# Key lookup by TensorE, gates written in eight pieces, a later choice and a rounded output projection in one transformer step

## The chip, the cores and the metric

One core of a Trainium2 chip runs the whole program. The metric is device time in microseconds (us) of one execution.

## The reference, cut to what matters

There are 640 tokens: 128 of a prompt and 512 latent ("sample") tokens, in five blocks of 128; block 0 is the prompt. Each group goes through one layer: normalisation and modulation, an input projection, differential attention (half of the width) and Fourier mixing (the other half), an output projection into the residual, and then a retrieval over 16384 single-neuron experts.

```python
x = x + g1 * mixer_merge(att, four, subln_g, lam_init, w_out)   # m @ w_out, m of 1024 columns
h2 = rmsnorm(x, norm2_g) * (1 + sc2) + sh2
q = (hf @ w_query).reshape(T, N_PEER_HEADS, 2, PEER_KEY_DIM // 2)
s = jnp.einsum('thpk,hpnk->thpn', q, sub_keys)
s1, i1 = lax.top_k(s[:, :, 0], PEER_TOPK)
s2, i2 = lax.top_k(s[:, :, 1], PEER_TOPK)
cand = s1[..., :, None] + s2[..., None, :]
top_s, pos = lax.top_k(cand.reshape(T, 8, 256), PEER_TOPK)
idx = (i1 * 128 + i2) at pos
g = softmax(top_s)
a = gelu(einsum('tkd,td->tk', expert_u[idx], hx))
out = einsum('tk,tkd->td', g * a, expert_v[idx])
```

Every token thus picks 16 experts for each of 8 heads, 128 in all, each named by two keys of 128 (i1, the row of the expert table, and i2, the column).

## The kernel before

Engines are named PE (TensorE), DVE (VectorE), ACT (ScalarE), POOL (GpSimd) and SP (SyncE, which issues most transfers). Each engine has its own program, written out by hand in order, and they meet at semaphores (`s_...`). The stages of the profiled execution:

- **Modulation and input projection** (0 to 209 us). The projection `z` is done in three products of rounded numbers: a number is split into `hi` (rounded to the type fp32r) and `lo` (the rest), and hi*hi, hi*lo and lo*hi are summed (L1599, L1600, L1603). The output projection is not done so: it is one plain f32 product.
- **Fourier mixing** (209 to 235): eight units; ACT copies each result into `mixT`.
- **Attention** (235 to 311): 20 iterations, one for each block and head, the prompt's four first. DVE takes maxima (L1132), scales and combines; ACT does exponentials and, in `att_out`, copies the turned output into `mixT` (L798); POOL does a `pow` for each block.
- **Merges** (311 to 386). `merge(b, half)` on PE (L1758) multiplies block b of `mixT` with a half (512 columns) of the output weights, 8 matmuls for each of ten pairs. DVE multiplies the result with the gate (L1192) and adds it to X (L1194); ACT squares X for the norm (`square2`, L824); DVE prepares the variance (`make_h2`, L1180), POOL raises it to the power (L512), and DVE makes h2 in two operations (L1182, L1184). PE turns h2 (`turned`, L1767), ACT rounds it (`turned_high`, L837) and DVE takes the rest (`turned_low`). The order is staggered: blocks 0 to 2 are merged wholly before the first turn. Meanwhile the query weights are split: ACT `query_high` (L830), DVE `query_low` for chunks 0 and 1 (L1208), POOL for 2 and 3 (L586).
- **Query projection and key scores** (386 to 554). PE runs `products3` (L1784 to L1786). DVE finds the top 16 keys of each head and side (`key_tops`). POOL builds a table `curve` in L590.
- **Choice of block 1** (554 to 568), then **three gate blocks** starting at 568.24, 612.62 and 657.04 and ending at 706.8. For the three dense blocks (ORDER is 1, 2, 3, 4, 0; the first three are dense) the gates of all 16384 experts are laid out as a matrix in memory (`gates_scratch`). For 32 groups of four tokens (quads), PE forms differences between token keys and all keys (`differences`, L1860), ACT makes them a one-hot operand (`one_hot`, L867), DVE makes the other operand (`gate_rows`, L1386; every fourth on POOL, L557), PE multiplies them (`dense_gates`, L1873), and ACT copies the result out (L905). SP sends half a block at a time to memory; of the last half, first 8 of 64 pairs (512 KB) and then the other 56 in one transfer (3584 KB).
- While block n is laid out, DVE also **chooses** for the next one (`choose`): sums of pairs (L1255), candidates, ranks (`select`). The keys at the ranks are looked up so: `is_equal` against all ranks gives a one-hot (L1350), a multiplication puts the index in (L1352), and a tree of additions over 16 places sums it up (L1356, L1357), once for each side. DVE then writes the key, its square and the rest of its square as `key2` (L1360 to L1363). PE spreads these in `stack_fill` (after quad 24 of the block before), ACT copies them (`stack_out`, p of 25), PE turns keys and gates (`selT_fill`, after quad 27; ACT `sel_out` at p of 28).
- **Into the experts** (706.8 to 739.5). DVE chooses for the prompt (`choose(4, 0, 0, 0, (0, 0))`); SP loads the first gates back; the pipeline of expert pairs starts up.
- **Experts** (to 1765), 128 steps: for the dense blocks, PE computes scores of 128 experts against 384 tokens (`U_hi`, `U_lo`), ACT the gelu, DVE multiplies with the gates (L1441), and PE the product with V (L1784 to L1786 again). The other two blocks (4 and the prompt) are done by POOL, which fetches rows one by one (L537), and DVE, which multiplies them (L1459, L1470). X, spilled to memory before, comes back in the course of it, and a tail ends the program.

Lines that the text touches, as they stand before:

```python
            choose(0, 0, 0, 0, (0, 0))
            choose(1, 1, 2, 3, (2, 6))
            choose(2, 2, 2, 3, (2, 6))
            choose(3, 3, 2, 3, (2, 0))
```

The numbers in `choose` say how many quads of the running block DVE does between the parts of a choice: 18 before `gate_weights` and 6 behind it.

Of the kernel before, what the change touches and what calls it, by code (L numbers as in the profile page):

```python
# [15 lines left out]
H = 4  # L16
# [21 lines left out]
SPARSE = (4, 0)  # L38
RPB = 4
# [12 lines left out]
GCUT = (0, 8, PAIRS)  # L52
# [21 lines left out]
def _phase1_jobs():  # L74
# [18 lines left out]
    for i, u in enumerate(units):  # L93
        jobs += [(("fa",) + u, "act"), (("fb",) + u, "dve")]
        if i:
            jobs.append((("fmix",) + units[i - 1], "act"))
    jobs.append((("fmix",) + units[-1], "act"))
# [4 lines left out]
def _phase2_jobs():  # L102

    order = ["m0", "m1", "m2", "T0", "m3", "T1", ("merge", 4, 0), "T2", ("merge", 4, 1), "T3", "T4"]
    jobs = []
    for o in order:
        if isinstance(o, tuple):
            jobs.append((o, "dve"))
        else:
            kind = "merge" if o[0] == "m" else "h2T"  # L110
            jobs += [((kind, int(o[1]), half), "dve") for half in range(2)]
    return jobs
# [19 lines left out]
def program(nc, xall, condT, w_mod, b_mod, norm1_g, w_in, lam4, subln_g, w_fourier, w_out, norm2_g,  # L132
# [7 lines left out]
    with ctx:  # L140
# [41 lines left out]
        with ExitStack() as over:  # L182
# [8 lines left out]
            wq_lo_first = laid("wq_lo_first", [P, KD, NC], f32r)  # L191
        w_hi = [w_hi_first] + [w_hi_next] * (IN_CH - 1)
# [20 lines left out]
        mixT = cutout(WO + WRING * KD * NC, 5120).rearrange("p (k t) -> p k t", k=KD)  # L213
# [7 lines left out]
        wq_in = [cutout(CO + 10240, KD * NC).rearrange("p (k n) -> p k n", k=KD)] + [chunk[:, r] for r in (0, 2, 1)]  # L221
        wq_hi = [wq_hi_even, wq_hi_odd] * 2
        wq_lo = [wq_lo_first[:, :, :]] + [w_lo[:, r] for r in (0, 2, 1)]
# [5 lines left out]
        onehot = cutout(BO + 4096, 1024).bitcast(bf16).rearrange("p (j s) -> p j s", j=TOPK)  # L229
# [15 lines left out]
        square = cutout(BO + 4096, P)  # L245
# [75 lines left out]
        s_arstd = sem("s_arstd"); s_att = sem("s_att"); s_attT = sem("s_attT"); s_mix = sem("s_mix")  # L321
        s_fill2 = sem("s_fill2"); s_h2hi = sem("s_h2hi"); s_dve2 = sem("s_dve2")
# [5 lines left out]
        s_selT = sem("s_selT"); s_selfill = sem("s_selfill"); s_diff = sem("s_diff"); s_key2 = sem("s_key2"); s_stackfill = sem("s_stackfill"); s_stack = sem("s_stack"); s_curve = sem("s_curve"); s_tab = sem("s_tab"); s_lhs1 = sem("s_lhs1"); s_rhs1 = sem("s_rhs1"); s_rhs1p = sem("s_rhs1p")  # L328
# [14 lines left out]
        DFT_C = MOD_CH + IN_CH  # L343
        OUT_C = DFT_C + 1
        CHUNKS = OUT_C + OUT_CH
# [20 lines left out]
        def _(sp):  # L366
# [23 lines left out]
            sp.wait_ge(s_mix, NBLK)  # L390
# [37 lines left out]
            for b in range(1, NDEN + 1):  # L428
                for half in range(2):
# [12 lines left out]
                    for r in range(len(GCUT) - 1):  # L442
                        pairs = slice(GCUT[r], GCUT[r + 1])
                        sp.dma_start(to[:, pairs], held[:, pairs]).then_inc(s_gpart[r], 16)
# [20 lines left out]
            load_pairs(1, GCUT[1] // 2)  # L465
            sp.wait_ge(s_gpart[1], 16)
            sp.wait_ge(s_spill, 16 * NBLK)
            at = [GCUT[1] // 2] + [2 * NBLK + 3 * b for b in range(NBLK + 1)] + [TWICE]
            for b in range(NBLK + 1):
                load_pairs(at[b], at[b + 1])  # L470
                if b < NBLK:
                    sp.dma_start(XF[:, b], x1_d[b * P:(b + 1) * P, :]).then_inc(s_xf, 16)
                else:
                    sp.dma_start(fing, final_g.unsqueeze(0).broadcast_to([P, D])).then_inc(s_fing, 16)
# [1511 lines left out]
```

## Time and profile before

| | us |
|---|---|
| median of three runs | 1820.45 (1818.86 to 1822.13) |
| the profiled execution | 1815.94 |
| its span (first to last instruction) | 1813.9 |
| mean granted clock of TensorE | 0.966 of full speed |

Rows of a timeline give the start, the duration and the instruction (a run of alike ones is one row with its count), and in brackets how long the engine was idle before it and what released it. Groups by line give busy time, mean ns of one, and idle time before. A row by source gives minimum, median and maximum ns. The window rows give, for each engine, its busy time and the number of instructions in the stretch.

### The profile page before, as it was taken

The page shows a single profiled execution, that of the slowest core. Times are in us where ns is not written, and L with a number is a line of the kernel's source. Part 1 is how long each engine was busy: PE and PEld are TensorE (multiplying, and loading weights), DVE is VectorE, ACT ScalarE, POOL GpSimd, SP SyncE. Part 2 cuts the span into 40 slices and gives each one's busy share as a digit, 9 for nine tenths or more (in the row PEclk, how much of TensorE's full clock was granted, in tenths as well). Part 3 has the DMA queues.
Part 4 walks back from the last instruction along what each step waited for, and adds up shares of the span by engine and source line. Part 5 has one row for each costly group of instructions (what it writes and reads, how often), then busy time and mean ns, then how long its engine had stood idle before and what let it go on. Part 6 is the DMA issues. An engine that isn't in the chain of part 4 may idle for free.

```text
span 1813.9 us, 28223 instructions
## 1 busy us (share of the span) xinstructions
PE 1665.3 (92%) x9322; PEld 1442.0 (79%) x9338; DVE 1506.1 (83%) x3069; ACT 645.6 (36%) x1085; POOL 916.1 (51%) x771
## 2 busy tenths in 40 slices
PE   4999998999954886899999999999999999999994
PEld 2776766479953886799999999999999999999993
DVE  0732266457999999799999999999999999999997
ACT  1212266121103785233333333333333333333331
POOL 1101000013402665777778877777666666666661
PEclk9999999999976998999999999999999999999997
DMA  9445202140010668999999999999999999999993
GB/s 355 173 163 208 75 1 98 42 184 3 1 47 1 187 186 253 385 406 409 407 408 390 402 409 409 409 409 409 409 408 409 409 409 403 410 409 407 406 397 124
DMA packets 198137, 518.28 MB, mean 286 GB/s; under 512 B 14643, under 2 KB 64435, under 8 KB 197941
## 3 DMA queue, kind: packets, MB, share of 16 engines
q0 software_dynamic: 73728, 268.47, 37.3%
q1 hardware_dynamic: 122320, 245.59, 36.3%
q10 hardware_dynamic: 2022, 3.38, 0.5%
q8 instruction: 36, 0.59, 0.1%
q14 instruction: 31, 0.25, 0.0%
HBM read 486.45 MB, written 30.93 MB: 285 GB/s over the span
## 4 chain that ended last, share of the span: by engine, by line
PE 79%; DVE 10%; DMA 5%; issue 3%; ACT 3%; POOL 0%; SPq 0%; POOLq 0%; ACTq 0%; DVEq 0%; PEldq 0%; another core or an unknown queue 0%
PE ps L1786 20%; PE ps L1785 20%; PE ps L1784 19%; PE ps L1758 4%; PE ps L1873 4%; DMA arena_w<-in_w_mod 2%; PE ps L1599 2%; PE ps L1603 2%; PE ps L1600 2%; PE ps L1697 2%; DMA arena_w<-in_w_in 1%; ACT arena_w L867 1%; DVE arena L1470 1%; PE ps L1721 1%; DVE arena L1307 1%
## 5 line engine op out<-in xcount | busy, mean ns | idle before, releaser
L1786 PE MATMUL ps<-hT_hi,U_lo 128*128 128x384 f32 x1024 | 344.3, 336 | 0.0
L1784 PE MATMUL ps<-hT_hi,U_hi 128*128 128x384 f32 x1024 | 344.1, 336 | 0.0
L1785 PE MATMUL ps<-hT_lo,U_hi 128*128 128x384 f32 x1024 | 343.5, 335 | 0.0
L537 POOL DMA_INDIRECT rows_under<-in_expert_u,idxn x192 | 273.8, 1426 | 116.4 <-issue 41.8
L1784 PE MATMUL ps<-hT_hi,C_hi 128*128 128x512 f32 x768 | 301.2, 392 | 14.5 <-DVE C_lo L1447 14.5
L537 POOL DMA_INDIRECT rows_under<-in_expert_v,idxn x192 | 242.7, 1264 | 140.4 <-DVE arena L1470 77.8
L1786 PE MATMUL ps<-hT_hi,C_lo 128*128 128x512 f32 x768 | 303.2, 395 | 0.0
L1785 PE MATMUL ps<-hT_lo,C_hi 128*128 128x512 f32 x768 | 303.1, 395 | 0.0
L1470 DVE SCALAR_TENSOR_TENSOR arena<-rows_under,dots,arena 128x1024 f32<-128x1024 f32 x192 | 247.8, 1291 | 4.8
L930 ACT ACTIVATE act_t<-ps 128x384 f32<-128x384 f32 x128 | 63.0, 492 | 386.2 <-PE ps L1786 386.2
L1784 PEld LDWEIGHTS ps<-hT_hi,U_hi 128*128 128x128 f32 x1024 | 192.6, 188 | 4.9
L1785 PEld LDWEIGHTS ps<-hT_lo,U_hi 128*128 128x128 f32 x1024 | 192.4, 188 | 4.9
L892 ACT CAST hT_hi<-arena 128x1024 fp32r<-128x1024 f32 x128 | 135.0, 1055 | 170.7 <-PE ps L1786 170.6
L1786 PEld LDWEIGHTS ps<-hT_hi,U_lo 128*128 128x128 f32 x1024 | 192.3, 188 | 0.0
L1784 PEld LDWEIGHTS ps<-hT_hi,C_hi 128*128 128x128 f32 x768 | 145.6, 190 | 42.9 <-DVE C_lo L1447 15.6
L1408 DVE TENSOR_TENSOR U_lo<-U_in,U_hi 128x1024 fp32r<-128x1024 f32 x128 | 156.3, 1222 | 21.5 <-ACT U_hi L885 21.2
L1786 PEld LDWEIGHTS ps<-hT_hi,C_lo 128*128 128x128 f32 x768 | 145.2, 189 | 30.7
L1785 PEld LDWEIGHTS ps<-hT_lo,C_hi 128*128 128x128 f32 x768 | 145.3, 189 | 27.7
L885 ACT CAST U_hi<-U_in 128x1024 fp32r<-128x1024 f32 x128 | 134.1, 1048 | 80.7 <-DMA U_in<-in_expert_uT 80.4
L1413 DVE TENSOR_TENSOR hT_lo<-arena,hT_hi 128x1024 fp32r<-128x1024 f32 x128 | 155.8, 1217 | 2.9 <-ACT hT_hi L892 2.8
L557 POOL TENSOR_SCALAR arena<-iota,arena 128x128 f32<-128x128 f32 x96 | 90.8, 955 | 127.7 <-ACT arena L876 81.0
L1459 DVE SCALAR_TENSOR_TENSOR rows_under<-rows_under,arena_w 128x1024 f32<-128x1024 f32 x96 | 116.0, 1220 | 7.7 <-DMA rows_under<-in_expert_u,idxn 7.7
(273 smaller groups left out, 3010.9 us busy)
## 6 DMA issues: line engine op xcount, KB each, us to landing
U_in<-in_expert_uT SPq DMA_DIRECT2D x128, 512.0 KB, 8.7
arena<-in_expert_v SPq DMA_DIRECT2D x128, 512.0 KB, 6.5
arena_w<-in_w_mod SPq DMA_DIRECT2D x12, 2048.0 KB, 12.4
gate_in<-gates_scratch SPq DMA_DIRECT2D x62, 384.0 KB, 7.9
gates_scratch<-arena_w SPq DMA_DIRECT2D x5, 4096.0 KB, 16.6
arena_w<-in_w_in SPq DMA_DIRECT2D x4, 2048.0 KB, 8.7
arena_w<-in_w_query SPq DMA_DIRECT2D x4, 2048.0 KB, 10.8
arena_w<-in_w_out SPq DMA_DIRECT2D x2, 2048.0 KB, 8.4
```

Source lines behind the costliest of these rows:

```text
L537: pool.indirect_dma_start(out=rowr[row], out_offset=None, in_=table, in_offset=bass.IndirectOffsetOnAxis(ap=idxn[:, g, row:row + 1], axis= ...
L557: ins = pool.tensor_scalar(rhs1[AIDED][:, t, :], iota[:, :], selT[:, b % 2, 0, at:at + 1], selT[:, b % 2, 1, at:at + 1], ALU.is_equal, ALU ...
L885: act.copy(U_hi[:, r], U_in[:, r]).then_inc(s_uhi, 1)
L892: act.copy(V_hi[r], V_in[:, r].rearrange("p (k n) -> p k n", k=KD)).then_inc(s_vhi, 1)
L1408: dve.tensor_tensor(U_lo[:, r], U_in[:, r], U_hi[:, r].bitcast(f32), ALU.subtract).then_inc(s_ulo, 1)
L1413: dve.tensor_tensor(V_lo[r], V_in[:, r].rearrange("p (k n) -> p k n", k=KD), V_hi[r].bitcast(f32), ALU.subtract).then_inc(s_vlo, 1)
L1459: dve.scalar_tensor_tensor(out=rowr[q], in0=rowr[q], scalar=1.0, in1=h2row[k], op0=ALU.mult, op1=ALU.mult, accum_out=dst).then_inc(s_used, 1)
L1470: dve.scalar_tensor_tensor(out=accS[:, k], in0=rowr[q], scalar=c, in1=accS[:, k], op0=ALU.mult, op1=ALU.add).then_inc(s_used, 1)
L1758: last = nc.tensor.matmul(out, mixT[:, k, b * P:(b + 1) * P], chunk[:, (OUT_C + half) % WRING, k, :], start=(k == 0), stop=(k == KD - 1))
L1784: nc.tensor.matmul(out, hi, rhi, start=start, stop=False)
L1785: nc.tensor.matmul(out, hi, rlo, start=False, stop=False)
L1786: return nc.tensor.matmul(out, lo, rhi, start=False, stop=stop)
```

## The change

1. **Output projection in three rounded products.** `mixT` becomes `mix_hi` and `mix_lo`, the weights `wo_hi` and `wo_lo`; PE does 24 matmuls for each `merge` in place of 8. New work: ACT `out_high` (16 casts, eight of them in the prompt's four attention iterations), POOL `out_low` (8 before the attention's `pow`s, 8 behind), DVE `mix_low` (8, after the Fourier units) and `att_low` (5, in the attention loop; PE waits for it). All first halves are merged before any second half; a block's h2 is made after its second half. `query_low` of chunk 0 moves from DVE to POOL, and the load of chunk 0 waits for the first five merges.
2. **Key lookup on PE.** For the first four choices the tree of additions gives way to `pick`: 16 accumulating matmuls of 128 x 128 x 128 in bf16 with a unit matrix, once for each side, after quads 16 and 21 of the block. ACT makes the squares (`key_squares`, after quad 23), DVE only the rest (`finish`, ahead of its last 6 quads, waiting for ACT's `s_keysq`). `stack_fill` comes two quads later.
3. **Gates in pieces.** The last half block is written in eight transfers of 512 KB; only the first goes out at once, the others between the loads of turns 2 to 18 of the expert loop. POOL's third row fetch waits for one gate load less. The loads that bring X back come a turn or two earlier.
4. **The prompt's choice parted.** Its candidates and first side stay ahead of the experts; its second side and its weights move into the first expert step.

```diff
-GCUT = (0, 8, PAIRS)
+GCUT = tuple(range(0, PAIRS + 1, 8))
+SENT = {1: 2, 2: 4, 3: 6, 4: 8, 5: 12, 6: 15, 7: 18}
+BACK = {0: 9, 1: 11, 2: 14, 3: 17, 4: 20, NBLK: 23}
...
-    order = ["m0", "m1", "m2", "T0", "m3", "T1", ("merge", 4, 0), "T2", ("merge", 4, 1), "T3", "T4"]
...
+    jobs = [(("merge", b, 0), "dve") for b in range(NBLK)]
+    for b in range(NBLK):
+        jobs.append((("merge", b, 1), "dve"))
+        jobs += [(("h2T", b - 1, half), "dve") for half in range(2 if b else 0)]
+    jobs += [(("h2T", NBLK - 1, half), "dve") for half in range(2)]
...
-        mixT = cutout(WO + WRING * KD * NC, 5120).rearrange("p (k t) -> p k t", k=KD)
+        mix_hi = HT_lo
+        mix_lo = HT_hi[:, :, :].rearrange("p k t -> p (k t)").rearrange("p (b k t) -> p b k t", b=NBLK, k=KD)
+        wo_hi = [w_lo[:, DFT_C % WRING], wq_lo_first[:, :, :]]
+        wo_lo = [w_lo[:, (OUT_C + half) % WRING] for half in range(OUT_CH)]
...
+            sp.wait_ge(s_fill2, NBLK)
             sp.dma_start(wq_in[0], w_query_v[:, :, 0:NC]).then_inc(s_wq[0], 16)
             for b in range(NBLK):
-                sp.wait_ge(s_x1, 2 * (b + 1))
+                sp.wait_ge(s_x1, NBLK + b + 1)
...
+                    sp.dma_start(to[:, 0:GCUT[1]], held[:, 0:GCUT[1]]).then_inc(s_gpart[0], 16)
+            def send_part(r):
+                pairs = slice(GCUT[r], GCUT[r + 1])
+                sp.dma_start(gates_d[pairs, :, 2 * NDEN - 1].rearrange("m p e t -> p m (e t)"),
+                             gbuf[:, 1].rearrange("p (m e) t -> p m (e t)", e=2)[:, pairs]).then_inc(s_gpart[r], 16)
...
+            turn = 1
+            for at in sorted(set(SENT.values()) | set(BACK.values())) + [TWICE]:
+                for r in range(1, len(GCUT) - 1):
+                    if turn < 4 * r < at:
+                        load_pairs(turn, 4 * r)
+                        turn = 4 * r
+                    if turn == 4 * r:
+                        sp.wait_ge(s_gpart[r], 16)
+                load_pairs(turn, at)
+                turn = at
+                for r in SENT:
+                    if SENT[r] == at:
+                        send_part(r)
...
+            def out_low(half):
+                src = chunk[:, (OUT_C + half) % WRING]
+                for k in range(KD):
+                    pool.wait_ge(s_ohi, KD * half + k + 1)
+                    pool.tensor_tensor(wo_lo[half][:, k, :], src[:, k, :], wo_hi[half][:, k, :].bitcast(f32),
+                                       ALU.subtract).then_inc(s_olo, 1)
...
+            out_low(0)
             for b in range(NBLK):
                 pool.wait_ge(s_avar, b + 1)
                 pool.tensor_tensor(ss4[:, 1, :], ss4[:, 0, :], powe[:, 0:H], ALU.pow).then_inc(s_arstd, 1)
+            out_low(1)
             for b in range(NBLK):
+                if b == NBLK - 1:
+                    query_low(0, range(2 * b - 2, 2 * b))
...
                 if first and row == 2:
-                    for part in s_gin:
-                        pool.wait_ge(part, 16)
+                    pool.wait_ge(s_gin[0], 16)
...
                 if ci == 2:
+                    pool.wait_ge(s_qfill, 16)
...
+                for k in ks:
+                    act.copy(wo_hi[half][:, k, :], chunk[:, i % WRING, k, :]).then_inc(s_ohi, 1)
...
+                if i < KD // 2:
+                    out_high(0, range(2 * i, 2 * i + 2))
+            out_high(1, range(KD))
...
+            for b in range(1, NBLK):
+                if b == NBLK - 1:
+                    act.wait_ge(s_fill2, B2.pos["merge", b, 1] + 1)
+                    query_high(0, range(2 * b - 2, 2 * b))
+                square2(b)
+                turned_high(b - 1)
+                if b < NBLK - 1:
+                    query_high(0, range(2 * b - 2, 2 * b))
+            turned_high(NBLK - 1)
...
+            def key_squares(n):
+                act.wait_ge(s_picked, 2 * n + 2)
+                if n:
+                    act.wait_ge(s_stackfill, n)
+                    act.wait_ge(s_key2, n)
+                act.copy(key2[:, 0, :], ps[:, 0, 256:384]).then_inc(s_keysq0, 1)
+                act.activation(square, ps[:, 0, 256:384], ACT.Square).then_inc(s_keysq0, 1)
+                act.wait_ge(s_keysq0, 2 * n + 2)
+                act.copy(key2[:, 1, :], square).then_inc(s_keysq, 1)
...
+                    key_squares(b)
+                if b < NDEN and p == 27:
...
+                src = bank1("fmix", s, g)
+                dve.wait_ge(s_fhi, units.index(u) + 1)
+                if s == 0:
+                    dve.tensor_tensor(mix_lo[:, 0, 4 + g, :], src[:, 0:P], mix_hi[:, 4 + g, 0:P].bitcast(f32),
+                                      ALU.subtract).then_inc(s_dve1, 1)
+                else:
...
+                if i:
+                    mix_low(units[i - 1])
+            mix_low(units[-1])
...
+            def att_low(b):
+                dve.wait_ge(s_mix, b + 1)
+                dve.scalar_tensor_tensor(out=mix_lo[:, b, 0:4, :], in0=ps[:, 7, :].rearrange("p (h t) -> p h t", h=H),
+                                         scalar=lam[:, 7:8], in1=mix_hi[:, 0:4, b * P:(b + 1) * P].bitcast(f32),
+                                         op0=ALU.mult, op1=ALU.subtract).then_inc(s_mixlo, 1)
...
+            dve.wait_ge(s_out, 32)
+            for b in range(NBLK):
+                merge(b, 0)
+            for b in range(NBLK):
+                merge(b, 1)
+                var2(b)
+                if b:
+                    turned_low(b - 1)
+                make_h2(b)
+            turned_low(NBLK - 1)
...
+            def picked(n, ws, bd=0, share=(0, 0, 0, 0)):
+                b = ORDER[n]
...
+                    if n and n < LATE_PICK:
+                        dve.wait_ge(s_picked, 2 * n - 1 + w)
...
+                    eqs = dve.tensor_tensor(o4, o4, idxf[:, w].unsqueeze(2).broadcast_to([P, TOPK, TOPK, PH]), ALU.mult)
+                    if n < LATE_PICK:
+                        eqs.then_inc(s_eqs, 1)
+                        gate_quads(bd, share[2 * w + 1])
+                        continue
...
+            def finish(n):
                 if n < NDEN:
...
-                    link(dve.tensor_copy(key2[:, 1, :], square))
+                    dve.wait_ge(s_keysq, n + 1)
                     dve.tensor_tensor(key2[:, 2, :], square, key2[:, 1, :], ALU.subtract).then_inc(s_key2, 1)
...
+                candidates(n, bd, pairs_share)
+                picked(n, (0, 1), bd, (select_share,) * 4)
                 gate_quads(bd, weights_share[0])
                 gate_weights(n)
+                finish(n)
                 gate_quads(bd, weights_share[1])
...
+            candidates(4, 0, 0)
+            picked(4, (0,))
+            def first_row(i, q):
+                if i == 0 and q == 2:
+                    picked(4, (1,))
+                    gate_weights(4)
+                dot_row(0)(i, q)
...
-                    pe.wait_ge(s_mix, b)
+                    pe.wait_ge(s_mixlo, b)
...
+                    if b == 0:
+                        pe.wait_ge(s_olo, KD * half + k + 1)
+                    last = products3(out, mix_hi[:, k, b * P:(b + 1) * P], mix_lo[:, b, k, :],
+                                     wo_hi[half][:, k, :], wo_lo[half][:, k, :], k == 0, k == KD - 1)
...
+            for b in range(NBLK):
+                merge(b, 0)
+            for b in range(NBLK):
+                merge(b, 1)
+                if b:
+                    turned(b - 1)
...
+            def pick(n, w):
...
+                if n and w == 0:
+                    pe.wait_ge(s_selT, n)
+                if n and w == 1:
+                    pe.wait_ge(s_keysq, n)
+                for j in range(TOPK):
+                    if w == 0 and n < NDEN:
+                        last = nc.tensor.matmul(ps[:, 0, 0:P], onehots[0][:, j, :], identb, start=(j == 0), stop=(j == TOPK - 1))
+                    else:
+                        at = 256 if w else 384
+                        last = nc.tensor.matmul(ps[:, 0, at:at + P], identb, onehots[w][:, j, :],
+                                                start=(j == 0), stop=(j == TOPK - 1))
+                last.then_inc(s_picked, 1)
...
+            pick(0, 0)
+            pick(0, 1)
...
+                if q % QUADS in (16, 21):
+                    pick(q // QUADS + 1, (q % QUADS - 16) // 5)
+                if q % QUADS == 26 and q // QUADS + 1 < NDEN:
```

## Rows read from the trace of the kernel before

**Rows 1.** The page: its first line and the busy time of each engine.
```profile
span 1813.9 us, 28223 instructions
...
PE 1665.3 (92%) x9322; PEld 1442.0 (79%) x9338; DVE 1506.1 (83%) x3069; ACT 645.6 (36%) x1085; POOL 916.1 (51%) x771
```
**Rows 2.** Busy time in four windows: attention, merges, first gate block, experts.
```profile
core 0: us, PE busy (x) PEld busy (x) DVE busy (x) ACT busy (x) POOL busy (x), PEclk, DMA share, GB/s
240.00:300.00 60.00, 57.21 (x355) 44.06 (x355) 53.01 (x108) 44.47 (x134) 3.54 (x3) 0.96 0.00 1
311.06:385.90 74.84, 74.84 (x193) 34.81 (x193) 31.48 (x45) 11.72 (x22) 2.17 (x4) 0.96 0.15 57
568.24:612.62 44.38, 39.17 (x284) 35.08 (x289) 41.33 (x145) 33.74 (x65) 29.04 (x32) 0.91 0.34 96
1300.00:1350.00 50.00, 50.00 (x254) 45.55 (x253) 48.90 (x50) 18.12 (x25) 31.64 (x27) 1.00 1.03 408
```
**Rows 3.** PE's timeline: products of the merges, rounded products of the input projection.
```profile
start us, us, engine line op out<-in xcount [idle before <-releaser]
...
311.06 44.11 PE L1758 MATMUL ps<-arena_w 128*128 128x512 f32 x96 [0.78 <-ACT arena_w L800]
...
185.68 0.39 PE L1599 MATMUL ps<-w_hi_next,HT_hi 128*128 128x512 f32 x1
...
208.57 0.39 PE L1603 MATMUL ps<-w_lo,HT_hi 128*128 128x512 f32 x1
```
**Rows 4.** Timeline, DVE and ACT at the end of the merges.
```profile
385.31 0.69 DVE L1192 TENSOR_TENSOR arena_w<-ps,arena 128x512 f32<-128x512 f32 x1 [3.82 <-PE ps L1758]
...
386.75 1.06 ACT L824 ACTIVATE arena_w<-arena 128x1024 f32<-128x1024 f32 x1 [7.68 <-DVE arena L1194]
...
388.74 1.34 DVE L1182 SCALAR_TENSOR_TENSOR arena_w<-arena,rstd 128x1024 f32<-128x1024 f32 x1 [0.65 <-POOL rstd L512]
...
390.11 1.31 DVE L1184 TENSOR_TENSOR arena_w<-arena_w,arena 128x1024 f32<-128x1024 f32 x1
```
**Rows 5.** Timeline of POOL and DVE at 439 us; L1255 and L586 by source.
```profile
439.16 7.03 POOL L590 TENSOR_TENSOR arena_w<-ident,arena_w 32x4096 bf16<-32x4096 f32 x1
...
442.10 4.14 DVE L1255 TENSOR_TENSOR arena<-arena 128x32 f32<-128x32 f32 x1
...
L1255 DVE TENSOR_TENSOR arena<-arena x20: 163/171/4145, 442.1 to 702.4; 128x32 f32<-128x32 f32 x20
...
L586 POOL TENSOR_TENSOR w_lo<-arena_w,wq_hi_even x8: 1281/1288/1301, 424.3 to 437.8; 128x512 fp32r<-128x512 f32 x8
```
**Rows 6.** Groups of instructions by line, the whole span.
```profile
L1062 DVE TENSOR_TENSOR HT_lo<-ps,HT_hi 128x512 fp32r<-128x512 f32 x10 | 6.4, 682 | 0.7 <-ACT HT_hi L684 0.7
...
L867 ACT ACTIVATE arena_w<-ps 128x512 f32<-128x512 f32 x96 | 58.3, 608 | 0.4 <-PE ps L1860 0.2 <-remote 0.2
...
L905 ACT COPY arena_w<-ps 128x512 f32<-128x512 f32 x96 | 56.5, 589 | 31.7 <-PE ps L1873 30.3
...
L1356 DVE TENSOR_TENSOR arena<-arena 128x1024 bf16<-128x1024 bf16 (+2 forms) x30 | 14.8, 494 | 0.8
```
**Rows 7.** Timeline of the second gate block, 612 to 658 us.
```profile
623.24 1.71 PE L1873 MATMUL ps<-arena_w 128*128 128x128 f32 x8 [2.69 <-issue]
...
625.16 1.92 PE L1873 MATMUL ps<-rhs_more,arena_w 128*128 128x128 f32 x8
...
633.38 4.45 POOL L557 TENSOR_SCALAR arena<-iota,arena 128x128 f32<-128x128 f32 x4 [1.33 <-PE ps L1873]
...
635.39 0.31 ACT L880 ACTIVATE arena<-arena 128x128 f32<-128x128 f32 x1
...
647.57 2.14 DVE L1386 TENSOR_SCALAR arena_w<-iota,arena 128x128 f32<-128x128 f32 x8
...
648.28 1.05 PE L1873 MATMUL ps<-arena,arena_w 128*128 128x128 f32 x8
...
649.38 1.05 PE L1873 MATMUL ps<-arena_w 128*128 128x128 f32 x8
```
**Rows 8.** The way into the experts: DVE and PE timeline, and one DMA issue.
```profile
719.21 0.56 DVE L1441 TENSOR_TENSOR act_t<-act_t,gate_in 128x384 f32<-128x384 f32 x1 [1.28 <-DMA gate_in<-gates_scratch]
...
739.49 0.67 PE L1784 MATMUL ps<-hT_hi,C_hi 128*128 128x512 f32 x1 [4.55 <-DVE C_lo L1447]
...
gates_scratch<-arena_w SPq DMA_DIRECT2D x1, 3584.0 KB, 22.2
```

More of the change, by code:

```diff
@@ L38 @@
 SPARSE = (4, 0)
+LATE_PICK = 4
 RPB = 4
@@ L95, in _phase1_jobs @@
         if i:
-            jobs.append((("fmix",) + units[i - 1], "act"))
-    jobs.append((("fmix",) + units[-1], "act"))
+            jobs.append((("fmix",) + units[i - 1], "dve"))
+    jobs.append((("fmix",) + units[-1], "dve"))
     return jobs
 def _phase2_jobs():
-    order = ["m0", "m1", "m2", "T0", "m3", "T1", ("merge", 4, 0), "T2", ("merge", 4, 1), "T3", "T4"]
[L105 to L111, printed above, removed]
+    jobs = [(("merge", b, 0), "dve") for b in range(NBLK)]
[3 more added lines that the diff above has]
+    jobs += [(("h2T", NBLK - 1, half), "dve") for half in range(2)]
     return jobs
@@ L894, in _ @@
             share_exps(0)
+            key_squares(0)
             stack_out(1)
@@ L1169, in _ @@
                     att_norm(i // H - 2)
+                if i % H == 2 and i > 2 * H:
+                    att_low(i // H - 2)
             def bank2(*name):
@@ L1749, in bank2, with products3 @@
                 return ps[:, i % 8, :]
-            pe.wait_ge(s_mix, NBLK)
+            pe.wait_ge(s_mixlo, NBLK)
             pe.wait_ge(s_exp, 2 * len(UNITS))
-            chunk_ready(OUT_C)
-            chunk_ready(OUT_C + 1)
+            def products3(out, hi, lo, rhi, rlo, start, stop):
+                nc.tensor.matmul(out, hi, rhi, start=start, stop=False)
+                nc.tensor.matmul(out, hi, rlo, start=False, stop=False)
+                return nc.tensor.matmul(out, lo, rhi, start=False, stop=stop)
             def merge(b, half):
@@ L1757, in merge @@
                 for k in range(KD):
-                    last = nc.tensor.matmul(out, mixT[:, k, b * P:(b + 1) * P], chunk[:, (OUT_C + half) % WRING, k, :],
-                                            start=(k == 0), stop=(k == KD - 1))
+                    if b == 0:
+                        pe.wait_ge(s_olo, KD * half + k + 1)
+                    last = products3(out, mix_hi[:, k, b * P:(b + 1) * P], mix_lo[:, b, k, :],
+                                     wo_hi[half][:, k, :], wo_lo[half][:, k, :], k == 0, k == KD - 1)
                 last.then_inc(s_fill2, 1)
@@ L1848, in selT_fill @@
                     pe.wait_ge(s_selT, b - 1)
-                for w, src in enumerate((sel[:, 0, :], gates[:, 1, :])):
-                    last = nc.tensor.transpose(ps[:, 0, w * P:(w + 1) * P], src, ident[:, :])
-                last.then_inc(s_selfill, 1)
+                nc.tensor.transpose(ps[:, 0, P:2 * P], gates[:, 1, :], ident[:, :]).then_inc(s_selfill, 1)
             def differences(q):
```

195 lines of the change are left out of this document (85 added, 110 removed).

## The prediction

> **What bounds the kernel now.** I read the page first. The span is 1813.9 us, PE is busy for 92% of it and DVE for 83% [rows 1]; a share like this is a mean over stages, so the windows come next. In the experts PE never idles (50.00 of 50.00 us), and DMA is at a share of 1.03 and DVE at 48.90 of 50 [rows 2]: there only PE work removed would count, and the change removes none. What it touches are the stages ahead. In attention PE is busy for 57.21 of 60 us and DVE for 53.01; in the merges PE for all of 74.84 us and DVE for only 31.48; in the first gate block of 44.38 us, PE for 39.17 and DVE for 41.33, so neither is full and the waits between them decide [rows 2]. The timelines of single engines in these stretches then give the durations.
>
> **1. Attention and Fourier.** The change puts eight DVE operations behind the Fourier units; all but the last stand in DVE's gaps there, and the last is ahead of the first scores: one PSUM operation of 512 columns, 0.68 us [rows 6], +0.8 with its wait. `att_low` is five of that kind. Three stand in a loop in which DVE is idle 7 of 60 us: between 0 and 2.0, I take +1.0. One stands in the tail, where PE waits for it: +0.75. ACT's eight casts (0.61 each by the nearest row, 512 columns) stand in the prompt's short iterations: 4.9 us of work in a stage in which ACT is idle for 15 of 60; 0 to 3, I take +0.7. POOL's first eight `out_low` cost nothing as work (POOL is busy 3.54 of 60 us), but look at the rows around 442 us: while POOL's L590 ran from 439.16 to 446.19, DVE's L1255, usually 0.171 us, took 4.14 and ended just as POOL did [rows 5]. An operation of DVE on two SBUF inputs stood still until POOL's was over. Eight POOL operations of 1.29 us [rows 5] therefore can stop DVE eight times, by 0 to 10.3 us in all; on average a stop would be less than half an operation and not all meet such a DVE operation: +3.0 (0 to 7). Sum +6.25.
> The Trainium skill ("SBUF — State Buffer", section "SBUF: two separate sides") says that DVE and GpSimd share a pair of ports and that whichever starts first has it for the whole instruction, DVE only where it runs in a two-port mode or has two SBUF inputs. By that rule the maxima and other PSUM readers of the loop go on beside POOL, and this term would be nearer to +2; the trace agrees in the 4.14 us of an operation with two SBUF inputs.
>
> **2. Merges.** The 96 records of plain f32 are six halves of 16 (two records a matmul) and take 44.11 us [rows 3]; a half in the stage's steady part is 6.87 us, 0.43 a record, so that about 2.75 is the slow start. The rounded ones start every 0.2266 us: 101 intervals from 185.68 to 208.57 [rows 3]. 24 of them are 5.44 us for each half in place of 6.87. PE alone would need 10 x 5.44 + 4 x 0.9 (turns) + 2.75 = 60.8 us against 74.84. But the new order gives every block a chain behind its second half: from the multiplication at 385.31 over the square (1.06) and the variance to the end of h2 (1.34 + 1.31, done at 391.42) it is 6.1 us [rows 4]. I take 6.1 for the first and, with `turned_low` of the block before in between, about 7.0 for the next three, where PE needs 6.4. So: 2.75 + 6 x 5.44 = 35.4 to the end of the sixth half, then 6.1 + 3 x 7.0 and the last turn, 63.8 in all: -11.0. Against this, POOL now does `query_low` of chunk 0 (2 x 1.29 for each block) while DVE makes h2 out of two SBUF inputs, the very pairing of the 4.14 us row: 0 to 9, I take three stops of 1.6 and a last of 0.7, +5.5. Net -5.5. Below -11 it can't come unless the chain is shorter than its rows.
>
> **3. Key stage.** Its work is the same. `query_low` of chunk 0 leaves DVE, and L590 comes later, with the same stop of DVE somewhere else (4.14 before). I take 0 (-2 to +4).
>
> **4. Gate stage.** The trees are 30 additions of 0.494 us [rows 6], six a choice, 3.0 us; with the last sum and the four key operations, each near the 0.31 of a 128-column one [rows 7], about 4.7 us of DVE for each choice. In the first choice PE is idle and DVE alone sets the pace: 4.7 less, and two picks, three ACT steps of 0.31 and hops more. A pick is 16 matmuls of 128 columns. A quad's eight f32 records of 128 columns take 1.05 us [rows 7], 0.13 each; a rounded matmul takes about half of a plain record (0.2266 to 0.43 above), so a pick is 1.05 to 2.1, and below that if bf16 is quicker still (0.9). I take 1.1 warm and twice that in this cold stretch. Net -1.0 (-1.6 to -0.6).
> The Trainium skill ("TensorE: Matmul & The Clock Gate", section "Wait — 56ns, not 53.3ns?") gives 55.6 ns for such a matmul at 2.4 GHz and 106.7 at 1.2; by it a pick would be 0.9 or 1.7 us, and the sum would stand within 0.5.
>
> In blocks 1 and 2 the gain doesn't arrive. Quads 11, 15, 19, 23 are bounded by POOL's own operand, made in up to 4.45 us [rows 7] after PE has freed a buffer; two picks of 1.1 fill what the trees leave. So quad 23 ends about when it does now, at 649.3. Now quad 24 starts at once, at 649.38 behind 648.28 [rows 7], since DVE had its operand ready. After the change DVE may not start this operand until `finish`, and `finish` waits for ACT's `key_squares`, which stand behind quad 23: ACT copies the result (0.59), makes a one-hot (0.61) [rows 6], then three steps of 0.31; DVE 0.3, then the quad's operand, half of the 2.14 us for two [rows 7], 1.07. That is 3.6 us with the overlap of the first two, plus 0.1 of a hop. Queued behind the waiting DVE are its last six quads and the next block's first, and PE waits for each. A gap of 2.69 us left the two next groups at 1.71 and 1.92 us in place of 1.05 [rows 7], which is the lower level of the clock, 1.2 GHz: +1.45 in two. Together +5.0 for each of two blocks (3.3 to 6). In block 3 `finish` waits for the picks alone, and the splits stand behind it: +1.5. Stage: +10.5.
>
> **5. Into the experts.** The first gates are used at 719.21, released by their load, and the second product with V starts at 739.49 after waits of PE [rows 8]. The load ran beside a transfer of 3584 KB that took 22.2 us [rows 8]; this goes, and the parted choice takes about 5 us of DVE out of the way, of which most comes back inside the first step. What then is late is DVE's chain of splits: I follow it to 17.6 us where it is 20.3 between the two rows, -2.7, and -2.3 for the load. -5.0 (-7 to -2).
>
> **6. Experts.** PE paces them, and the second part of the choice stands in a step in which DVE has a few us to spare. The seven pieces are 3584 KB, at 409 GB/s about 9 us of a DMA that is full [rows 2]; their cover is the loads' lead of a turn or more: 0, and +9 if that lead is gone.
>
> **Sum.** 6.25 - 5.5 + 0 + 10.5 - 5.0 = +6.25. The profiled execution took 1815.94 and would take 1822.2; it is 4.5 below the median of 1820.45, which becomes 1826.7.
>
> **Rivals.** (a) The gate blocks get shorter. If the chain behind quad 23 is covered, because operands for 24 and on are ready or ACT runs ahead, PE's work sets the block: 39.17 + 2.2 for the picks = 41.4 against 44.38, -3.0 in place of +5.0, twice: 1826.7 - 16 = 1810.7, faster. It decides once operand 24 is there by the end of 23. For it: DVE falls from 41.33 to about 36.6 us of the block. Against: the order of DVE's program. (b) The stops by POOL cost nothing, as both engines mostly read other operands: -3.0 - 5.5, so 1818.2. For it: among 20 L1255 one alone was slow [rows 5]. (c) DMA has no lead: +9, so 1835.7; the share of 1.03 speaks for it, PE's full 50 us against.
>
> **Chances.** Forecast 0.50 (own range 1820 to 1834), (a) 0.17, (b) 0.18, (c) 0.10, other 0.05. What can be told from no change is 0.2%, 3.6 us. The forecast lies 2.6 above that edge, so 0.40 of its 0.50 is slower and 0.09 within; (a) is nearly all faster; (b) is 0.06 faster, 0.09 within, 0.03 slower; (c) slower. That makes faster 0.24, within 0.20, slower 0.56. The range of 1809 to 1837 reaches from (a) to (c).
>
> **What would show it.** Merges: 24 matmuls in 5.44 us, a stage near 69 us, DVE rows of h2 over 1.34 beside POOL's 1.29. Gates: a PE idle of about 3 us before quad 24, released by DVE, and a period near 49 us; if the period is 41, (a) is right. Transition: PE's start on the second product with V less than 28 us after the end of the gates. Experts: 8.28 us a step as now. The prediction fails most easily at quad 24.

## Result and profile after

The changed kernel takes 1846.57 us (median of four runs, 1844.16 to 1856.2) against 1819.65 for the kernel before in the same runs; the ratio is 1.0162, with a 95% interval of 1.0141 to 1.0182. The forecast was 1826.7 with a range of 1809 to 1837: the sign was right and the size was not. Between the two profiled executions the difference is larger, 32.8 us where +6.25 was forecast, because the one before lies 3.7 us under that median and the one after 2.0 over its own.

The span of the profiled execution is 1846.7 us; it was 1813.9. The page's first line and its chain of work that ended last, by engine:

```profile
span 1846.7 us, 28485 instructions
...
PE 1680.0 (91%) x9525; PEld 1476.6 (80%) x9543; DVE 1506.1 (82%) x3035; ACT 651.8 (35%) x1110; POOL 947.7 (51%) x795
...
PE 56%; DMA 16%; DVE 15%; issue 7%; ACT 3%; POOL 2%; SPq 1%; DVEq 0%; POOLq 0%; another core or an unknown queue 0%; ACTq 0%; PEldq 0%
```

DMA is now 16% of the chain, where it was 5%. I cut both traces at the same five events of PE and took differences:

| stretch | before | after | difference | forecast |
|---|---|---|---|---|
| start to first product of the merges | 311.06 | 320.94 | +9.9 | +6.25 |
| merges, to the first query product | 74.84 | 68.16 | -6.7 | -5.5 |
| query, keys and first choice, to the first turn of gates | 181.21 | 179.10 | -2.1 | -1.0 |
| three gate blocks | 139.91 | 149.61 | +9.7 | +11.5 |
| into the experts, to the second product with V | 32.47 | 27.58 | -4.9 | -5.0 |
| from there to the end | 1074.41 | 1101.31 | +26.9 | 0 |

The first five sum to +5.9, for which +6.25 was forecast. The whole miss is the last line. The windows there (us, then busy time and count of PE, PEld, DVE, ACT and POOL, granted clock, DMA share, GB/s) answer to the last of [rows 2]:

```profile
740.00:790.00 50.00, 45.69 (x224) 40.86 (x222) 42.28 (x66) 15.56 (x22) 38.39 (x30) 0.97 0.98 376
1110.00:1160.00 50.00, 46.09 (x219) 41.15 (x218) 42.02 (x64) 15.35 (x21) 32.46 (x25) 0.93 0.98 379
1320.00:1370.00 50.00, 45.90 (x219) 41.20 (x218) 43.23 (x43) 14.88 (x21) 27.94 (x25) 0.93 0.98 382
```

Before, PE never idled between 740 and 1350 us. Now it loses 4 us in each window, and in the second and third its granted clock is 0.93. (In the first, 3.1 of the 4.3 us are still the way in: the second product with V starts at 745.39.) One such place, followed through the timelines of SP, ACT, DVE and PE, and then four windows of 4 us. U is the block of expert weights that a step loads; `U_hi` is its rounded part, made by ACT, and `U_lo` the rest, made by DVE; `C_hi` and `C_lo` are the same of the gated scores:

```profile
772.43 0.39 SPq L454 DMA_DIRECT2D gates_scratch<-arena_w  x1
773.19 0.69 SPq L423 DMA_DIRECT2D U_in<-in_expert_uT  x1
...
788.53 1.05 ACT L947 CAST U_hi<-U_in 128x1024 fp32r<-128x1024 f32 x1 [7.43 <-DMA U_in<-in_expert_uT]
789.48 0.51 ACT L999 CAST C_hi<-act_t 128x384 fp32r<-128x384 f32 x1
...
789.60 1.23 DVE L1517 TENSOR_TENSOR U_lo<-U_in,U_hi 128x1024 fp32r<-128x1024 f32 x1 [5.45 <-ACT U_hi L947]
...
792.50 0.50 PE L1872 MATMUL ps<-hT_hi,C_hi 128*128 128x512 f32 x1 [3.70 <-DVE C_lo L1564]
```

```profile
784.00:788.00 4.00, 4.00 (x24) 3.92 (x23) 0.16 (x2) 0.00 (x0) 3.03 (x4) 1.00 1.02 409
788.00:792.00 4.00, 0.80 (x5) 0.47 (x3) 2.40 (x4) 2.79 (x4) 0.00 (x0) 1.00 1.03 415
792.00:796.00 4.00, 3.50 (x10) 2.80 (x11) 4.00 (x7) 0.13 (x1) 2.91 (x2) 0.70 0.99 370
796.00:800.00 4.00, 4.00 (x19) 3.49 (x18) 4.00 (x7) 2.38 (x3) 3.39 (x3) 0.88 1.01 399
```

Read it upwards. PE is said to wait for `C_lo`, but DVE was idle from 784 to 788 (0.16 of 4 us): it stood at `U_lo`, which is ahead of `C_lo` in its program, for ACT's `U_hi`, and ACT had stood 7.43 us for the load of U. That load was issued at 773.19, in the same queue, right behind the piece sent at 772.43. After the idle, the granted clock is 0.70 and 0.88 in the next two windows: PE's first products still take 0.39 us, then those from 793.92 to 796.48 take 0.63, the lower of its levels, 1.2 GHz, and then it is back at 2.4. There are five such idles behind seven pieces, 3.70, 3.18, 3.91, 1.62 and 4.10 us, 16.5 in all. The same 610 us of experts, after and (from 740) before:

```profile
745.00:1355.00 610.00, 593.10 (x2940) 536.54 (x2941) 557.64 (x815) 207.62 (x279) 441.33 (x321) 0.98 1.01 396
```

```profile
740.00:1350.00 610.00, 610.00 (x3077) 555.29 (x3076) 582.02 (x840) 217.59 (x293) 455.51 (x332) 1.00 1.02 406
```

16.9 us are idle. PE has 2940 matmul records where it had 3077, which is 27.2 us of work at the old pace; so the other 10.3 us went into slower matmuls, and a mean clock of 0.98 (0.975 to 0.985) would take 9 to 15. The stalls and the slower work behind them make up the 26.9.

### The profile page after: what moved, and what is told of

Same layout as the page of the kernel before. It is cut to its first block, busy times and chain, and to the rows that moved or that the text cites. A ratio compares the mean times of both kernels' runs of the same rounds, so it can differ in the third digit from the quotient of the medians.

```text
span 1846.7 us, 28485 instructions
## 1 busy us (share of the span) xinstructions
PE 1680.0 (91%) x9525; PEld 1476.6 (80%) x9543; DVE 1506.1 (82%) x3035; ACT 651.8 (35%) x1110; POOL 947.7 (51%) x795
## 4 chain that ended last, share of the span: by engine, by line
PE 56%; DMA 16%; DVE 15%; issue 7%; ACT 3%; POOL 2%; SPq 1%; DVEq 0%; POOLq 0%; another core or an unknown queue 0%; ACTq 0%; PEldq 0%
PE ps L1872 13%; PE ps L1873 13%; PE ps L1874 13%; DMA U_in<-in_expert_uT 9%; PE ps L2000 4%; PE ps L1716 2%; PE ps L1720 2%; PE ps L1717 2%; DMA arena_w<-in_w_mod 2%; PE ps L1814 2%; POOL rows_under L583 2%; DMA arena_w<-in_w_in 1%; DVE hT_lo L1522 1%; DVE arena L1587 1%; DVE rows_under L1576 1%
## 5 line engine op out<-in xcount | busy, mean ns | idle before, releaser
L583 POOL DMA_INDIRECT rows_under<-in_expert_u,idxn x192 | 284.6, 1482 | 126.5 <-issue 52.6
L603 POOL TENSOR_SCALAR arena<-iota,arena 128x128 f32<-128x128 f32 x96 | 85.8, 904 | 140.2 <-ACT arena L938 78.8
```

What stands on the lines that cost most here:

```text
L583: pool.indirect_dma_start(out=rowr[row], out_offset=None, in_=table, in_offset=bass.IndirectOffsetOnAxis(ap=idxn[:, g, row:row + 1], axis= ...
L603: ins = pool.tensor_scalar(rhs1[AIDED][:, t, :], iota[:, :], selT[:, b % 2, 0, at:at + 1], selT[:, b % 2, 1, at:at + 1], ALU.is_equal, ALU ...
```

## Experiments

Ratios are to the kernel before, run beside each; it took 1816.2 to 1817.4 us there, so times are compared by their ratios. Lines of edits are against the changed kernel unless said otherwise.

**Two transfers again.**

```diff
-GCUT = tuple(range(0, PAIRS + 1, 8))
-SENT = {1: 2, 2: 4, 3: 6, 4: 8, 5: 12, 6: 15, 7: 18}
+GCUT = (0, 8, PAIRS)
+SENT = {}
...
-                    sp.dma_start(to[:, 0:GCUT[1]], held[:, 0:GCUT[1]]).then_inc(s_gpart[0], 16)
+                    for r in range(len(GCUT) - 1):
+                        pairs = slice(GCUT[r], GCUT[r + 1])
+                        sp.dma_start(to[:, pairs], held[:, pairs]).then_inc(s_gpart[r], 16)
```

> The changed kernel with the last half block of gates written in two transfers again (512 KB, then 3584 KB, both at the end of the gates); the earlier loads of X, POOL's earlier fetch and the parted choice stay. Theory A, the seven written pieces make the U loads late in the experts: no wait of PE of 3 us or more is left between the second product with V and the tail, that stretch falls from 1101.3 us to about 1075, and the time to 1825 to 1831 (26.9 less, up to 4.9 given back on the way into the experts). Theory B, it is the earlier X loads or the parted choice in the first step: the waits stay and the time is 1841 or more.

Measured 1823.83 us, ratio 1.0043 (1.0029 to 1.0057): 1.19% or 21.6 us better than the change. From the second product with V to the end it is 1077.3 us, and ahead of 1785 us one idle of 0.40 us is left in the experts. The earlier loads of X (also 512 KB each, in the same queue) and the parted choice are still in it, so theory B falls. (The edit also drops two waits of SP for pieces; the run with small packets below costs as much without any.) The way into the experts is 30.1 us: of the 4.9 gained there, half came from the pieces.

**Pieces alone,** on the kernel before: the same constants, `send_part`, SP's loop and POOL's third fetch.

> The kernel before with nothing but the gates in pieces (eight transfers, the moved loads of X, POOL's third fetch). Theory A: the experts lengthen by some 27 us, the way into them shortens by 0 to 5, so 1841 to 1847. Theory B (it takes the parted choice or a later start of the experts): within 4 us of 1819.7. Priced by bytes alone at 409 GB/s it would be +9, 1829.

Measured 1839.84 us, ratio 1.0134 (1.0117 to 1.0151), +24.3 us. PE waits for `C_lo` seven times between 745 and 1400 us, 18.6 us in all, up to 6.5. The pieces cost this without any other part.

**Half as large, twice as many.**

```diff
-GCUT = tuple(range(0, PAIRS + 1, 8))
-SENT = {1: 2, 2: 4, 3: 6, 4: 8, 5: 12, 6: 15, 7: 18}
+GCUT = (0,) + tuple(range(8, PAIRS + 1, 4))
+SENT = {r: r + 1 for r in range(1, 15)}
```

> The changed kernel with the same 3584 KB written in 14 pieces of 256 KB, one at each of turns 2 to 15, in place of 7 of 512 KB. If each write has to be longer than the lead of the U loads to be felt (a threshold), half a piece costs little and the time is under 1830. If the cost goes by bytes or packets written, it stays at 1843 to 1850.

Measured 1835.77 us, 1.0116 (1.0098 to 1.0133): neither. Against two transfers it still costs 13 us, against the full pieces it saves 8, for the same bytes in the same packets. The waits are smaller and more, ten with 12.1 us in all in place of five with 16.5 (its profiled execution, 1830.3 us, is the fastest of its four). That fits a slack in each step, as DVE and ACT run a little ahead, which takes up part of each burst; this is argued, not shown. Pieces of this size are in any case not free.

**Seven writes that nothing needs,** on the kernel with two transfers and the covered quad of the next experiment. A transfer moves its bytes in packets; the size of a packet follows from how long the stretches are that lie together at both ends. First in rows of 4096 bytes:

```diff
+EXTRA = (2, 4, 6, 8, 12, 15, 18)
...
+                if at in EXTRA:
+                    r = EXTRA.index(at)
+                    sp.dma_start(extra_d[r * P:(r + 1) * P, :], G2[:, 0]).then_inc(s_extra, 16)
```

> The kernel with two transfers and covered quad 24 (0.9988 of the time before), and seven further writes of 512 KB at the turns 2, 4, 6, 8, 12, 15 and 18, ahead of the same U loads as the pieces, but to a scratch tensor that nothing reads, in rows of 4096 bytes. If the cost of a piece is its small packets of 512 bytes, these cost little: within 8 us of that kernel. If any write of 512 KB in that place is the cost, PE waits 2 to 4 us behind most of them and the time is 15 to 27 us longer.

and in packets of 512 bytes, the only difference being how the same tensor is cut (the places in memory that one packet after the other goes to change with it). SP waits for these writes only at the very end:

```diff
-                    sp.dma_start(extra_d[r * P:(r + 1) * P, :], G2[:, 0]).then_inc(s_extra, 16)
+                    sp.dma_start(extra_d[r * P:(r + 1) * P, :].rearrange("(m c) d -> m (c d)", m=8).rearrange("m (p e) -> p m e", p=P),
+                                 G2[:, 0].rearrange("p (m e) -> p m e", m=8)).then_inc(s_extra, 16)
```

> The same seven scratch writes at the same turns, with the same bytes, but in packets of 512 bytes as the pieces have. Packets as the cause: 15 to 27 us longer than the kernel without them, with PE waits of 2 to 4 us. If bytes or writing are the cause: the same as the run with rows of 4096 bytes, whatever that is.

Rows: 1822.5 us, ratio 1.0023 (1.0011 to 1.0035). Small packets: 1842.19 us, 1.0136 (1.0119 to 1.0154). The kernel without either is at 0.9988. So 3584 KB more in packets of 4096 bytes cost 0.35%, 6.4 us, close to the 9 that bytes at 409 GB/s give, and in packets of 512 bytes 1.48%, 26.9 us. The DMA line of the page, rows first and small packets second, has the same bytes, and they differ by 6272 packets, which is 7 x (1024 - 128):

```profile
DMA packets 199148, 521.99 MB, mean 286 GB/s; under 512 B 14755, under 2 KB 64547, under 8 KB 198949
```

```profile
DMA packets 205420, 521.99 MB, mean 284 GB/s; under 512 B 14755, under 2 KB 71715, under 8 KB 205221
```

The waits between 740 and 1400 us (us in total, times, the longest), again rows first:

```profile
ACT U_hi L948 <- DMA U_in<-in_expert_uT: 210.7, 78, 4.4
...
PE ps L1873 <- DVE C_lo L1565: 1.3, 3, 0.6
```

```profile
ACT U_hi L948 <- DMA U_in<-in_expert_uT: 135.1, 48, 9.4
...
PE ps L1873 <- DVE C_lo L1565: 19.1, 8, 5.7
```

ACT waits for U longer in total with rows, but never for more than 4.4 us, and of that PE has only 1.3 us of waits; with small packets single waits reach 9.4. Between 760 and 1350 us PE does 2980 matmuls in the kernel without the writes, 2955 with rows and 2838 with small packets: 4.9 and 28.1 us of work at 0.198 us each. So most of the price of rows is not in waits of PE but in matmuls that run a little slower at a granted clock of 1.00, and the traces don't say why.

**Quad 24 covered** (with two transfers):

```diff
-            choose(1, 1, 2, 3, (2, 6))
-            choose(2, 2, 2, 3, (2, 6))
+            choose(1, 1, 2, 3, (4, 4))
+            choose(2, 2, 2, 3, (4, 4))
```

> As the run before (two parts), and in blocks 1 and 2 DVE builds its operands of quads 24 and 25 before finish, not behind it (shares 4 and 4 in place of 2 and 6). If the 3.29 us idle of PE ahead of quad 24 is DVE waiting for ACT's squares, both idles go and the gate stage is 6.5 to 10 us shorter than with two parts alone. Rival, DVE is short of time anyway and the wait only moves to a later quad: within 2 us of it.

Measured 1814.78 us, ratio 0.9988 (0.9977 to 1.0), 10 us better than with two transfers alone. The gate blocks fall from 149.6 to 141.9 us, which is still 2 more than before the change; the other 2 us of the 10 lie in small differences of the rest. In the changed kernel the place looked so (timeline of ACT, DVE and PE):

```profile
605.53 0.27 ACT L927 CAST arena<-ps 128x128 bf16<-128x128 f32 x1
605.68 0.31 ACT L928 ACTIVATE arena<-ps 128x128 f32<-128x128 f32 x1
606.02 0.30 ACT L930 CAST arena<-arena 128x128 bf16<-128x128 f32 x1
606.35 0.41 DVE L1461 TENSOR_TENSOR arena<-arena 128x128 bf16<-128x128 f32 x1 [6.29 <-ACT arena L930]
606.68 2.18 DVE L1487 TENSOR_SCALAR arena_w<-iota,arena 128x128 f32<-128x128 f32 x8
...
608.04 1.13 PE L2000 MATMUL ps<-arena_w 128*128 128x128 f32 x8 [3.29 <-issue]
...
609.22 1.88 PE L2000 MATMUL ps<-arena_w 128*128 128x128 f32 x8
...
611.32 1.70 PE L2000 MATMUL ps<-rhs_more,arena_w 128*128 128x128 f32 x8
```

DVE idled 6.29 us for ACT's three steps, with six operands still to make. With two of them made ahead, the idle of 3.29 is gone from both blocks:

```profile
602.37 1.05 PE L1998 MATMUL ps<-arena_w 128*128 128x128 f32 x8
603.26 0.38 PE L1985 MATMUL ps<-arena_w,arena 128*128 128x512 bf16 x1
604.72 1.13 PE L1998 MATMUL ps<-rhs_more,arena_w 128*128 128x128 f32 x8 [1.08 <-ACT arena_w L917]
```

**No rounded projection** (with two transfers and the covered quad): all of part 1 as in the kernel before.

> The kernel with two transfers and covered quad 24, without the rounded output projection (plain f32 products, the old order of the merges). By the traces the projection costs 7 us in attention and gives 7 back in the merges: within 3 us of 0.9988 of the time before. If the products are worth more than that, it is slower by 4 us or more.

Measured 1815.95 us, 0.9992 (0.998 to 1.0005). With and without it the time is the same within what can be told: it costs ahead of the merges what it gives in them.

**POOL's operations and DVE.** First, the low part of query chunk 0 on DVE, two pieces behind each block's h2:

```diff
                 make_h2(b)
+                if b:
+                    query_low(0, range(2 * b - 2, 2 * b))
```

> The kernel with two transfers and covered quad 24, with the low part of query chunk 0 made by DVE (0.69 us each, two behind each block's h2) and not by POOL. If POOL's 1.29 us operations hold DVE up (h2 in 2.21 and 2.17 us where the first block has 1.28 and 1.22), those fall back to about 1.3 and the merges get 1 to 5 us shorter (1.9 less and 1.4 more for each of three blocks, and the last block's 0.8). If DVE was slow for another reason, they stay above 2 and the merges are 4 to 6 us longer.

Measured 1819.05 us, 1.0006 (0.9996 to 1.0017), 3.3 us worse than 0.9988 (0.9977 to 1.0); the two intervals just touch. The operations did fall back. DVE's h2 of the first and the second block in the changed kernel, and of the second with this edit:

```profile
359.69 1.28 DVE L1275 SCALAR_TENSOR_TENSOR arena<-arena,rstd 128x1024 f32<-128x1024 f32 x1 [0.66 <-POOL rstd L557]
...
366.46 2.21 DVE L1275 SCALAR_TENSOR_TENSOR arena_w<-arena,rstd 128x1024 f32<-128x1024 f32 x1
368.70 2.17 DVE L1277 TENSOR_TENSOR arena_w<-arena_w,arena 128x1024 f32<-128x1024 f32 x1
```

```profile
366.37 1.27 DVE L1269 SCALAR_TENSOR_TENSOR arena_w<-arena,rstd 128x1024 f32<-128x1024 f32 x1
367.68 1.23 DVE L1271 TENSOR_TENSOR arena_w<-arena_w,arena 128x1024 f32<-128x1024 f32 x1
...
392.71 1.52 DVE L1296 TENSOR_TENSOR w_lo<-arena_w,wq_hi_even 128x512 fp32r<-128x512 f32 x2
```

The merges got 2.4 us shorter (67.4 to 65.0), but the last pair of the chunk stood behind the last h2, done at 394; PE waited 5.1 us for it, and query, keys and first choice took 186.2 us where it is 179.1. (The profiled execution, 1825.0 us, is the slowest of its twelve.) So the pairs went into the gap in which DVE waits 1.22 us for ACT's square, and the last one ahead of the last h2:

```diff
                 merge(b, 1)
+                if b > 1:
+                    query_low(0, range(2 * b - 4, 2 * b - 2))
+                if b == NBLK - 1:
+                    query_low(0, range(2 * b - 2, 2 * b))
                 var2(b)
```

> As the run with the low part on DVE, but each pair of it stands where DVE waits for ACT's square of the next block anyway, and the last pair ahead of the last h2. If DVE's chain for each block sets the merges, its period falls from 8.65 us (POOL) and 7.96 (DVE, last pair behind) to about 6.7, the merges take 61 to 63 us, the query stage is not late at its first chunk, and the time is 4 to 6 us below the kernel with two transfers and covered quad 24: 0.9955 to 0.997 of before. If the late pair was not what cost 7 us of the query stage, it stays near 1.0006.

Measured 1810.21 us, 0.996 (0.9946 to 0.9974). The windows of the merges, with POOL first and with the slots second:

```profile
318.18:385.55 67.37, 62.12 (x273) 50.63 (x273) 33.25 (x38) 15.04 (x29) 23.48 (x19) 0.95 0.17 63
```

```profile
316.51:378.13 61.62, 60.43 (x272) 49.16 (x273) 29.99 (x42) 14.89 (x29) 12.37 (x12) 0.97 0.18 69
```

Four of DVE's eight new operations (2.6 us) lie in this window, and yet DVE is busy for 3.3 us less in it; the other four (2.5 us) follow right behind it, and the next stretch, up to the gates, is no longer than without them (178.8 us against 179.1). PE is nearly full.

**Short operations of POOL in attention** (on the kernel with two transfers and the covered quad; the low part of the first half's weights is left out of the result, and the high part stands in its place in the products):

```diff
-                    pool.tensor_tensor(wo_lo[half][:, k, :], src[:, k, :], wo_hi[half][:, k, :].bitcast(f32),
+                    c = slice(0, NC if half else 8)
+                    pool.tensor_tensor(wo_lo[half][:, k, c], src[:, k, c], wo_hi[half][:, k, c].bitcast(f32),
```

> The kernel with two transfers and covered quad 24, with POOL's eight operations of the first half of the weights cut to 8 of 512 columns; the products with that low part are done with the high part in its place (left out: the low part of the first half's weights). If these operations hold up DVE in the prompt's iterations, L1228 and L1229 fall from 0.70 and 0.58 us back to about 0.28 and 0.35 there and attention gets 2 to 4 us shorter. If ACT's casts or the added DVE work are the cost, attention stays within 1 us.

Measured 1809.72 us, 0.9964 (0.9948 to 0.998), 4.4 us less; this interval and that of the kernel it is built on (0.9977 to 1.0) just touch. The prompt's operations of DVE by group, with POOL's full operations first and short ones second:

```profile
L1226 DVE TENSOR_SCALAR arena<-arena,asum 128x128 f32<-128x128 f32 x4 | 2.8, 704 | 0.0
L1227 DVE SCALAR_TENSOR_TENSOR arena<-arena,asum 128x128 f32<-128x128 f32 x4 | 2.3, 578 | 0.1
```

```profile
L1228 DVE SCALAR_TENSOR_TENSOR arena<-arena,asum 128x128 f32<-128x128 f32 x4 | 1.4, 351 | 0.1
...
L1227 DVE TENSOR_SCALAR arena<-arena,asum 128x128 f32<-128x128 f32 x4 | 1.1, 277 | 0.0
```

Eight operations give back 2.6 us. The start of the merges in single profiles varies by 5.6 us between kernels that are alike up to there, so the 3.6 us by which it is earlier here doesn't settle it; the durations do, and the ratio points the same way.

**Third block too** (on the kernel with the slots): `choose(3, 3, 2, 3, (4, 0))` and then `gate_quads(3, 4)`.

> As the run with the low pairs in the slots, and in the third gate block DVE makes two more quads ahead of the splits of U and V (shares 4 and 4 in place of 2 and 6), where PE idles 3.2 us in every kernel so far. If DVE's order is the cause there too, the idle goes and it is 3 to 5 us faster than without; if the splits then are late for the experts, the gain is given back on the way into them: within 1.5 us.

Measured 1809.03 us, 0.9949 (0.9933 to 0.9965). The idle of 3.2 us ahead of quad 24 is gone, but waits of 1.63 and 0.57 stand close behind, the three blocks take 141.2 us where they took 141.0, and the way into the experts 30.1 in place of 31.4. The intervals of the two kernels overlap, so it isn't shown to be worth anything. This is the best version by its median, 0.5% below the kernel before.

## Why the prediction was right or wrong

**The step that failed is the sixth, "Experts".** It took 0 for the seven pieces, with +9 "if that lead is gone", from 3584 KB at 409 GB/s. Two things were wrong. The lead didn't cover: U loads stand in the same queue right behind each piece, and what a step can take up is some 4 us, as the run with rows suggests (ACT's waits up to 4.4 us, 1.3 us of PE's). And the price was that of bytes. It holds for packets of 4096 bytes (6.4 us measured); the gates go out in packets of 512, and the same bytes cost 26.9 us in them. [rows 8] already had a sign of this: those very 3584 KB took 22.2 us to land, not 9, and that row was used only for what its absence would give. The forecast took the gain of the piece that goes away from its own row and the cost of the pieces that come from another transfer's rate. Rival (c), given 0.10, named the mechanism with a third of the price; with the 22.2 us of the row the sum would have been 1849, but a time to landing beside other loads is not a price, and that it comes out so near is partly luck.

What the pieces gave on the way in, 2.5 of the 4.9 us, was real; they cost ten times that.

**Attention** was forecast at +6.25. The +9.9 of the profiled execution is too much: in eight other kernels with the rounded projection whole the merges begin between 315.2 and 320.8 us (318.0 on average), without it at 311.1, 312.1 and 311.9, so +6.3. With that in its place the first five differences would sum to +2.3, not to +5.9: that the sum of the table meets the forecast of +6.25 so well is luck. The stops by POOL, taken as +3.0, are 2.6 us in the two groups shown, or 4.4 by the ratio. **Merges:** -6.7 against -5.5. DVE's chain does set them. A block takes 8.65 us; 7.0 plus a stop of 1.6 was forecast. **Keys:** 0, and the first choice -2.1 where -1.0 was taken; its two picks took 1.86 and 1.89 us, for which 2.2 each was allowed. **Gate stage:** the wait at quad 24 is where it was put, 3.29 us in place of 3.6, and moving two operands in each of two blocks took 7.7 us out of the stage. The clock fell behind both idles, as forecast. In block 1 the quad right behind still took 1.13 us and the next two 1.88 and 1.70 (granted clock 0.50 from 610 to 612 us); in block 2 the quad right behind took 1.66 and the next 1.91. That is 1.5 us in two quads each time; the prediction's 1.45 was a small slip, as its own row gives 1.71 + 1.92 - 2 x 1.05 = 1.53. In block 3 PE idled 3.22 us as well, behind two splits of U and one of hT that DVE makes ahead of the operand, and three slow quads followed. Rival (a) was wrong, as DVE's order decides and not its load; even with the idles of blocks 1 and 2 gone the three blocks take 141.9 us against 139.9, so the lighter load of DVE gained nothing there. Rival (b) was wrong too: without the stops the time is 4.4 us shorter for attention and 5.1 us for the merges (0.9988 to 0.996), though DVE has the work of POOL to do there. **Into the experts** -4.9 for -5.0.

What stays open: how much of the 26.9 us is the clock alone, since no run here has the idles without it and the mean is rounded; why the same bytes and packets cost 13 us in pieces of 256 KB and 22 in pieces of 512; and whether it is the size of the packets itself that costs, or the scattered places in memory that small packets go to, since the two runs with scratch writes differ in both.

## What to carry to other kernels

Price a transfer by a run or a row with the same size of packets, not by the rate that larger packets reach in the same window; and where DMA is full, ask what stands behind it in its queue and how long the engines can do without. When work moves from a busy engine to an idle one, look for the instruction at which the busy one will now wait and move work that needs nothing ahead of it: here two quads moved in each of two blocks were worth 8 to 10 us. The same edit on the same engine gained 5 us or lost 3, depending only on whether it stood in a gap or behind the last thing that PE needed.

## What the runs showed of the hardware

A GpSimd operation with SBUF operands holds up VectorE operations beside it: 128x1024 on two SBUF inputs 2.21 us in place of 1.28, and, which I hadn't expected, also a TENSOR_SCALAR with one tensor input, 704 ns in place of 277. The Trainium skill ("SBUF — State Buffer", section "SBUF: two separate sides") names both kinds, two SBUF inputs and a two-port mode; both durations fit it, though no run here shows in which mode an operation ran. And 3584 KB of writes in a full DMA stage cost 26.9 us in packets of 512 bytes and 6.4 in packets of 4096, the same bytes sent at the same turns.
